# Heads' weight blocks before units', one period of 128 points, and the last piece of the first output block moved behind the second

## What is computed

```python
proj = jnp.einsum('btd,dc->btc', h, w_in[l])            # 4 * 1024 + 128 columns (rwkv), 4 * 1024 (hgrn)
o_rwkv = _rwkv7_branch(token_shift(proj[..., :RWKV_COLS]), ...)   # 16 heads of 64
o_hgrn = _hgrn2_branch(proj[..., RWKV_COLS:], ...)                # 8 heads of 128
y = jnp.einsum('btc,cd->btd', jnp.concatenate([o_rwkv, o_hgrn], axis=-1), w_out[l])
h = _layer_norm(ALPHA * h + y, ln_w[l], ln_b[l])
```

## Time and profile before

| | us |
|---|---|
| median of 3 runs | 3085.81 (3084.92 to 3086.78) |
| the profiled execution's own time | 3083.08 |
| its span | 3081.3 |
| TensorE busy in the span | 2990.8 (97%) |
| second block up to the second output block | 1789.11 to 2932.41 |

### The profile page before, as it was taken

One profiled execution on the slowest core, in us unless ns is written; L12 is line 12 of the kernel. 1 busy time (PEld: TensorE's weight loads), 2 busy tenths in 40 slices (PEclk: granted clock), 3 DMA queues, 4 the chain that ended last, 5 costly groups with the idle time before them and its releaser, 6 DMA issues.

```text
span 3081.3 us, 39125 instructions
## 1 busy us (share of the span) xinstructions
PE 2990.8 (97%) x15290; PEld 2418.7 (78%) x15290; DVE 1688.9 (55%) x2944; ACT 1244.6 (40%) x2150; POOL 284.5 (9%) x517
## 2 busy tenths in 40 slices
PE   8999999999999999999999999899999999999897
PEld 7778787787878887777778868787887887878786
DVE  6554545555543336566643364756666656564647
ACT  5443443434332335355442333344434343434422
POOL 0110101010100000000000011202112020212001
PEclk9999999999999999999999999999999999999999
DMA  4222222222234322222234322212223132224344
GB/s 166 78 81 83 83 77 82 83 82 76 83 127 144 105 89 70 77 74 70 75 137 140 104 90 70 84 62 78 90 63 98 55 92 66 80 76 143 132 130 157
DMA packets 86006, 288.97 MB, mean 94 GB/s; under 512 B 12080, under 2 KB 12720, under 8 KB 85568
## 3 DMA queue, kind: packets, MB, share of 16 engines
q1 hardware_dynamic: 69696, 243.66, 24.4%
q0 software_dynamic: 16128, 42.81, 4.5%
HBM read 261.13 MB, written 25.17 MB: 93 GB/s over the span
## 4 chain that ended last, share of the span: by engine, by line
PE 84%; DVE 8%; ACT 4%; issue 3%; DMA 1%; POOL 1%; DVEq 0%; SPq 0%; ACTq 0%; POOLq 0%
PE bank L280 15%; PE bank L282 14%; PE bank L281 14%; PE bank L284 7%; PE bank L286 7%; PE bank L285 7%; PE bank L1371 2%; PE bank L1302 1%; PE bank L1307 1%; PE bank L337 1%; PE bank L317 1%; DVE mc_split L735 1%; ACT mc_split L563 1%; PE bank L1282 1%; PE bank L466 1%
## 5 line engine op out<-in xcount | busy, mean ns | idle before, releaser
L280 PE MATMUL bank<-ma_split,mc_split 128*128 128x512 f32 x2304 | 956.3, 415 | 12.7 <-DVE ma_split L892 7.7
L735 DVE TENSOR_TENSOR mc_split<-mc,mc_split 128x1024 fp32r<-128x1024 f32 x434 | 535.2, 1234 | 783.4 <-ACT mc_split L563 782.4
L282 PE MATMUL bank<-ma_split,mc_split 128*128 128x512 f32 x2304 | 905.2, 393 | 0.0
L281 PE MATMUL bank<-ma_split,mc_split 128*128 128x512 f32 x2304 | 901.6, 391 | 0.0
L563 ACT ACTIVATE mc_split<-mc 128x1024 fp32r<-128x1024 f32 x434 | 457.5, 1055 | 650.6 <-PE bank L284 345.3
L280 PEld LDWEIGHTS bank<-ma_split,mc_split 128*128 128x128 f32 x2304 | 436.1, 189 | 121.2 <-issue 48.8
L282 PEld LDWEIGHTS bank<-ma_split,mc_split 128*128 128x128 f32 x2304 | 434.2, 188 | 97.0
L281 PEld LDWEIGHTS bank<-ma_split,mc_split 128*128 128x128 f32 x2304 | 436.6, 190 | 78.4 <-issue 4.2
L284 PE MATMUL bank<-mc_split,ma_split 128*128 128x512 f32 x576 | 230.2, 400 | 4.9 <-DVE mb L1781 3.4
L286 PE MATMUL bank<-mc_split,ma_split 128*128 128x512 f32 x576 | 225.3, 391 | 0.0
L285 PE MATMUL bank<-mc_split,ma_split 128*128 128x512 f32 x576 | 224.7, 390 | 0.0
(11 more groups left out here) (364 smaller groups left out, 3742.0 us busy)
## 6 DMA issues: line engine op xcount, KB each, us to landing
mc<-in_w SPq DMA_DIRECT2D x434, 512.0 KB, 3.5
x<-mc POOLq DMA_DIRECT2D x8, 1024.0 KB, 5.3
y<-mb_split SPq DMA_DIRECT2D x28, 256.0 KB, 2.5
ma_split<-y POOLq DMA_DIRECT2D x28, 256.0 KB, 4.4
mb<-in_xt SPq DMA_DIRECT2D x8, 512.0 KB, 9.0
mc<-in_x POOLq DMA_DIRECT2D x4, 1024.0 KB, 5.7
mc<-x POOLq DMA_DIRECT2D x4, 1024.0 KB, 8.1
mats<-mc POOLq DMA_DIRECT2D x32, 128.0 KB, 2.2
```

The source lines that it names most:

```text
L280: mm = pe.matmul(banks[j][:], wh[:, c], act_hi[:, kt, :], start=(kt == 0), stop=False)
L281: pe.matmul(banks[j][:], wl[:, c], act_hi[:, kt, :], start=False, stop=False)
L282: last = pe.matmul(banks[j][:], wh[:, c], act_lo[:, kt, :], start=False, stop=(kt == KT - 1))
L735: dve.tensor_tensor(w_low[:, s % NR, :, :], w_raw[:, s % NR, :, :], w_high[:, s % NH, :, :].bitcast(F32), ALU.subtract).then_inc(w_lo, 1)
```

## The change

It touches no product and no step's content. Four things move:

1. **Order of blocks.** Unit 0, `wa`, then head i and unit i + 1 in turn, then head 7: each head's block now stands ahead of the unit with the next number.
2. **Places of steps.** A unit's steps all begin at 128 u: prolog at 128 u + 10, V at + 32, G0 at + 42 (three points apart, before two), X at + 98, U0 at + 121, E0 at + 150. Before, prolog and chunks had periods of 128 and 120, so the distance between one unit's tail and the next unit's prolog shrank by 8 points a unit. A head's steps begin at 128 h + 65, 4.5 points apart, 4.0 for the last head (before 2.3 for head 6 and 2.0 for head 7).
3. **The first output block** has seven slots; its eighth, with the last unit's and last head's results, is a block of its own (`LATE`) behind the second output block. Its four banks are added by four more VectorE operations of 128 x 512.
4. **POOL's list.** Ten of the fourteen loads of earlier results (`y_loads`) stand ahead of the last unit's `sub_inverses`, and the rest, with two loads of the residual (`x2_load`), inside it.

```diff
-SLOT0 = [8 * b if b <= WA else 8 * b - 6 for b in range(BLOCKS)]
+LATE = OUT2 + 2
+BLOCKS = OUT2 + GROUPS + 1
+SLOTS = [2 if b == WA else 7 if b == OUT2 else 1 if b == LATE else 16 if b == BLOCKS - 1 else 8 for b in range(BLOCKS)]
+SLOT0 = [sum(SLOTS[:b]) for b in range(BLOCKS)]
...
-            KIND = [("rw", 0), ("wa", 0), ("rw", 1)]
-            for i in range(UNITS - 2):
-                KIND += [("hg", i), ("rw", i + 2)]
-            KIND += [("hg", i) for i in (UNITS - 2, UNITS - 1)] + [("out", n) for n in range(GROUPS)]
+            KIND = [("rw", 0), ("wa", 0)]
+            for i in range(UNITS - 1):
+                KIND += [("hg", i), ("rw", i + 1)]
+            KIND += [("hg", UNITS - 1), ("out", 0), ("out", 1), ("late", 0), ("out", 2), ("out", 3)]
...
-                i = k - CHUNKS
-                late = 0 if u else 5
+                i, begin = k - CHUNKS, 128 * u
                 if k < PART_B:
-                    return (128 * u - 54 if u else 7) + 2 * k
+                    return begin + 10 + 2 * k
                 if k < CHUNKS:
-                    return 120 * u + 16 + late + 2 * (k - PART_B)
-                begin = 120 * u + 26 + late
+                    return begin + 32 + 2 * (k - PART_B)
                 if i < 4:
-                    return begin + 2 * i
+                    return begin + 42 + 3 * i
                 if i < 13:
-                    return begin + 54 + 5 * (i - 4) // 2
+                    return begin + 98 + 5 * (i - 4) // 2
                 if i < CHUNK_K:
-                    return begin + 77 + 5 * (i - 13) // 2
-                return begin + 105 + 3 * (i - CHUNK_K)
+                    return begin + 121 + 5 * (i - 13) // 2
+                return begin + 150 + 3 * (i - CHUNK_K)
...
-                rate = {UNITS - 2: 23, UNITS - 1: 20}.get(h, 45)
-                return 64 * (BLOCK_OF["hg", h] + 1 - LANE0) + 1 + m * rate // 10
+                return 128 * h + 65 + m * (40 if h == UNITS - 1 else 45) // 10
...
+                    to = xr[0][:, t, :] if b == OUT2 else x3[:, t, n * N:(n + 1) * N]
+                    if b == LATE:
+                        dve.wait_ge(bank_free[t], freed(OUT2 + 1, t))
+                    dve.tensor_tensor(to, banks[t][:], xr[n % 2][:, t, :], ALU.add).then_inc(bank_free[t], 1)
...
+                if u == UNITS - 1:
+                    y_loads(pool, range(10, 12))
+                    pool.wait_ge(copies_ready, 2 * UNITS)
+                    for n in range(2):
+                        x2_load(pool, n)
...
+                for u in range(UNITS - 1):
+                    sub_inverses(pool, u)
+                y_loads(pool, range(10))
+                sub_inverses(pool, UNITS - 1)
```

More of the change, by code:

```diff
@@ L261, in swa_steps, with products @@
                 return [k for k in range(18) if swa_step_at(g, k) - 8 * s in points]
-            def products(pe, b, lhs_w, act_hi, act_lo, needs, slot0=None, tiles=range(4)):
-                for kt in range(KT):
-                    s = (SLOT0[b] if slot0 is None else slot0) + kt // 2
+            def products(pe, b, lhs_w, act_hi, act_lo, needs, slot0=None, tiles=range(4), kts=range(KT)):
+                for kt in kts:
+                    s = (SLOT0[b] if slot0 is None else slot0) + (kt - kts[0]) // 2
                     if kt % 2 == 0:
@@ L1152, in programs, with lane_steps @@
                     AT.setdefault(hg_at(u, m), ([], []))[1].append((u, m))
-            def lane_steps(b, points=range(8 * BLOCK_SLOTS)):
-                for point in points:
-                    rw, hg = AT.get(64 * (b - LANE0) + point, ((), ())) if b >= LANE0 else ((), ())
+            def lane_steps(b, points=None):
+                for point in range(8 * SLOTS[b]) if points is None else points:
+                    rw, hg = AT.get(8 * (SLOT0[b] - SLOT0[LANE0]) + point, ((), ())) if b >= LANE0 else ((), ())
                     yield from (("rw", u, k) for u, k in rw)
@@ L1416, in needs @@
                         if b == OUT2:
[L1417 to L1420, removed]
+                            pe.wait_ge(y_in[kt // 2], 64)
+                        if b == OUT2 + 1 and kt >= KT - 2:
+                            pe.wait_ge(y_rw_lo if kt == KT - 2 else y_h_lo, UNITS)
                     if kind == "wa":
@@ L1430, in second_pe @@
                         continue
-                    for point in products(pe, b, kind != "out", h_hi, h_lo, needs):
+                    kts = range(KT - 2) if b == OUT2 else range(KT - 2, KT) if kind == "late" else range(KT)
+                    for point in products(pe, b, kind in ("rw", "hg"), h_hi, h_lo, needs, kts=kts):
                         if b == RW0 and point % 8 == 3:
@@ L2017, in sub_inverses, with x2_load, y_loads @@
                 pool.wait_ge(xt_in, 16 * (u + 1))
[L2019 to L2028, removed]
+            def x2_load(pool, n):
+                pool.dma_start(xr[n % 2], a["x2"].rearrange("(t p) n -> p t n", p=P)[:, :, n * N:(n + 1) * N]
+                               ).then_inc(x2_in[n % 2], 16)
+                pool.dma_start(gb[n % 2], a["final_g"][:, n * N:(n + 1) * N].broadcast_to([P, N])).then_inc(x2_in[n % 2], 16)
+            def y_loads(pool, which):
+                for i in which:
+                    kt = Y_ORDER[i]
                     pool.wait_ge(w_free, SLOT0[OUT2 - 1] + i // 2 + 2)
@@ L2132 @@
     wa = w2[:, lo:hi].reshape(2, 8, P, P).transpose(0, 2, 1, 3).reshape(2, P, 2 * N)
-    parts = [w1, rw[0], wa, rw[1]]
-    for i in range(UNITS - 2):
-        parts += [hg[i], rw[i + 2]]
-    parts += [hg[UNITS - 2], hg[UNITS - 1], blocks(x["w_out_2"][0].reshape(KT, P, D)[Y_ORDER].reshape(D, D))]
-    parts.append(parts[-1][-BLOCK_SLOTS:])
+    parts = [w1, rw[0], wa]
+    for i in range(UNITS - 1):
+        parts += [hg[i], rw[i + 1]]
+    last = blocks(x["w_out_2"][0].reshape(KT, P, D)[Y_ORDER].reshape(D, D)).reshape(GROUPS, BLOCK_SLOTS, P, 2 * N)
+    parts += [hg[UNITS - 1], last[0, :-1], last[1], last[0, -1:], last[2], last[3], last[3]]
     w1 = np.concatenate(parts)
```

51 lines of the change are left out of this document (25 added, 26 removed).

## The result

The changed kernel takes 3120.85 us (median of 4 runs, 3120.24 to 3121.91), the kernel before 3086.3 beside it (4 runs, 3084.92 to 3090.56): ratio 1.0112 [1.0097, 1.0126]. It is slower, as forecast, but by 34.6 us and not by 16. The profiled execution took 3120.24 us with a span of 3117.8, so its span is 36.5 us longer than that of before.

The account below looks back on a forecast made before the run. TensorE, busy for 97% of the span, bounds the kernel; idle time and low clock go from 74 to 90 us, so 16 us on the profiled 3083.08 give 3099, and 2.7 for the median 3102 us; range 3092 to 3113.

Parts of the forecast that it names:

- seams: Points just behind a unit's block, where VectorE has take, tail and prolog at once; seven new ones, 10.9 us each, 76 us.
- Rival C: A unit's tail does not hold VectorE; seams keep only the wait behind the take: 47 us shorter, 3039; chance 0.08.
- rival A: Seams cost 3 us more each (late ScalarE split, POOL's list or one more bank claim): about 3123; chance 0.16.
- first half: the take: In each seam, O1 waits 1.9 us for VectorE's copy of U1, queued behind the take.
- second half: the tail: In each seam, TensorE's E3 waits 5.6 us for VectorE's E2 (44.6 less 39.0 us into the seam).
- the shared bank: The head's step 21, right behind E3, waits 0.9 us for the bank that ScalarE still reads.
- clock: Behind the waits of 5.6 and 0.9 us TensorE runs at 1.2 GHz for some 5 us: 2.5 us lost each seam.
- the inverse: X waits 1.2 us in each of eight units, 9.6 us; POOL's eight issues in the last inverse cost 1 us more.
- first unit: Eight more points between k7 and N, so the wait at N goes; 1 us stays.
- last head and last unit: At the end, 4.0 points a step with no prolog beside them: 1.5 us.
- the late piece: Four VectorE additions and a second pass of banks beside its 8 points: 0.5 us, 2 if something else holds VectorE.
- Idle in a new seam: Sum of three waits in one seam, at O1, E3 and step 21: 8.4 us, against 5.08 and 6.91 in two old ones.

Follow-up runs that it names:

- E0: No run but a kernel step, the first of a unit's tail (E0 to E5), VectorE work of 1.65 us in the prediction's replay.
- experiment 1: Changed kernel with E3 to E5 of units 0 to 6 eight points later: 3087.35 us, ratio 1.0006 to the kernel before.
- experiment 5: Changed kernel with the tail (E0 to E5) of units 0 to 6 behind the prolog and eight loads behind the last inverse: 3058.26 us, ratio 0.9907.
- experiment 6: Experiment 5 with U0 to O3 four points later, the last unit's tail beginning at + 154: 3047.68 us, ratio 0.9874.
- experiment 9: Experiment 6 with loads spread: six and the residual's ahead of the last inverse, four inside, four behind: 3044.21 us, ratio 0.9864.
- Experiment 3: Changed kernel with E0 and E1 on one eighth of their elements from the second unit on (result not the reference's): 3107.11 us, ratio 1.0074.
- experiment 4: Changed kernel with POOL's list as before the change, all loads of results behind the last inverse: 3150.18 us, ratio 1.0207.
- experiment 8: Changed kernel with the tail of units 0 to 6 five points later than in experiment 9's order of blocks, loads as in experiment 5: 3081.66 us, ratio 0.9988.
- experiment 10: Experiment 9 with U0 to O3 of units 0 to 6 nine points later than in the change, heads' step 15 three later: 3049.69 us, ratio 0.9881.
- 2: Changed kernel with E2 of every unit one point earlier: 3106.01 us, ratio 1.0064.

## Why the prediction was right in direction and wrong in size

The direction and the mechanism stand. The seams took what the end gave back, and the wait of E3 for E2 is the largest in the second block. Moving E3 away from E2 (experiment 1) removes the whole loss. Rival C, at 3039 for this kernel, was no error in kind: the same order of blocks comes near it once the tail does not meet the prolog (3058, 3048 and 3044 in experiments 5, 6 and 9), which the change did not do. The measured time lies beside rival A's 3123. Of the causes that A names, one was there, one more bank claim in a row (the wait at the head's step 20); ScalarE's split and POOL's list were not late.

The size was wrong by a factor of two. The prediction had 90 us of idle time and low clock after the change. The trace shows 82.5 us of waits, and the 36.5 us by which the span grew over 74 put the sum at 110, so some 28 us are low clock. The granted clock read directly says the same: in the second block up to the end of the late piece TensorE is busy for 57.3 us at 0.50, and half of that, 28.7, is lost (before: 32.3 us, 16.2 lost, where the prediction took 18). By the terms of the sum:

| term | forecast | measured | off by |
|---|---|---|---|
| *first half: the take*, O1, seven | 13.3 | 14.6 | + 1.3 |
| the head's step 20, seven | none | 10.1 | + 10.1 |
| *second half: the tail*, E3, seven | 39.2 | 38.3 | - 0.9 |
| *the shared bank*, seven | 6.3 | 6.1 | - 0.2 |
| *clock*, in seams | 17.5 | 23 | + 5.6 |
| *the inverse*, and POOL's issues | 10.6 | 5.1 | - 5.5 |
| *first unit* | 1 | 4.4 | + 3.4 |
| *last head and last unit* | 1.5 | 3.2 | + 1.7 |
| *the late piece* | 0.5 | 0.7 | + 0.2 |
| low clock outside the pattern of the seams | none | 5 | + 5 |

The wait at step 20 is half of the 20 us by which the prediction's 90 are short, and the two lines of the clock are the other half. The other lines cancel, which is luck: the inverse was put 5.5 us too high, and the first unit, O1 and the end as much too low.

**The step that failed** is "Idle in a new seam: 1.9 + 5.6 + 0.9 = 8.4 us": it counts three waits where there are four. The replay followed VectorE's queue up to E2 and compared with TensorE only there. Its own figures had step 19's update end at 35.1 and TensorE at E3 at 39.0. TensorE comes to step 20 four points and a step, 3.7 us, before E3 (2538.63 to 2542.33), so at 35.3, and needs ScalarE's copies, 0.6 us behind the update's end (2538.01 to 2538.63): a wait of 0.4 us was in the replay and was not read off. The old seam's 1.90 us was this very wait, one step further on, where E0 then stood ahead of the update; E0 was moved up, and its wait moved with it. Experiment 3 shows it: with E0 0.93 us shorter, this wait is 0.94 us shorter. The rest of the 1.4 is that VectorE was 1.3 us later than replayed: it waited 1.17 us for TensorE at step 18's update (2530.40, 28.8 into the seam instead of 27.3) and ended step 19's at 36.4. At E3 the two errors met: VectorE later by 1.4, TensorE by the wait of 1.4 and a little more, so the 5.6 us came out right by luck.

**Clock.** This is the second term that was too small. The step "2.5 us for each seam" was taken from behind a single wait of 6.40 us. Two waits, 5.5 and 0.9, with only E3's four short matmuls between them, keep the low level for 6.8 us, and it costs 3.3 us by experiment 9. In two of the seven seams it had fallen behind O1's wait of 2.1 us as well. The clock also fell outside seams, in the blocks from 2729.96 (0.98) and 2882.19 (0.95), behind waits of 3.8 and 3.2 us; the prediction gave those parts waits of 1.2 and 1.5 and no clock. Of the 57.3 us of busy time at 0.50, 47.6 lie in the seams and 9.75 in these two places, so 23.8 and 4.9 us are lost there.

**The inverse.** "A wait of 1.2 us for each of eight units" was taken from one unit's 0.50 and a window one point shorter. Only four of eight X waited, three by 0.7 us or less and one by 3.8 us, where the inverse took longer to land. The point less is free in most units.

**First unit.** The wait at N is 0.7 us, as forecast, but the next turn, B's, waits 2.8 us for VectorE and the first block starts 0.9 late. I had looked only at N.

**Right:** E3, the shared bank, O1, the late piece (0.7 us with the second output block's start; the third output block takes 43.62 us, 43.52 before), and POOL's eight issues beside the way of the blocks (the last unit's X waits 0.5 us). On the table load: ScalarE switches only once there, for E1 and not for k7. Behind this load, at 2539.12, ScalarE stood idle for VectorE for 3.43 us, and VectorE's split began 1.54 us behind the state update, as in before. Nothing is late by the 1.4 us of drain that the Trainium skill, "ScalarE: Activation LUTs", What ACT_TABLE_LOAD costs, adds to a switch, though idle time at this place could hide it. Behind the load of the earlier trace rows, where nothing could, there is none: the next operation starts 0.01 us later.

Open is why the inverse of the seventh unit lands late in some kernels (a wait of 3.4 to 3.8 us at its X in the changed kernel and in experiments 1, 4, 5, 8, 9 and 10, 0.7 us or less in 2, 3 and 6). In the changed kernel the last transfer of that inverse lands in 6.2 us, where the median is 4.7; no run says why. With the low clock behind it this wait is worth some 4 to 5 us between versions, an estimate, and experiment 9 has it where 6 has not.

## What to carry to other kernels

When steps of two lanes share an in-order engine, replay the whole meeting, and at every instruction of the waiting engine compare both clocks, not only at the one that looks worst; a wait that had disappeared at one step stood here at the step before. The distance between the points where one lane's tail and the next lane's prolog stand was worth more here than the work in them: the same operations cost 9.9, 4.8 to 6.4 or 3.1 us of TensorE's idle time with the tail 12, 17 or 26 points behind. When the order of blocks changes, ask which transfers in another engine's queue were timed by the old order: here that was worth 29 us.

## What the runs showed of the hardware

**Two short waits cost less clock than one of 2.4 us.** 1.3 and 1.6 us, 5.7 us apart, left the granted clock at 1.00 in six of seven seams (experiment 9). One of 2.4 us brought it down in six of seven seams (experiment 10) and cost up to 3.0 us more than the wait. 2.4 us at step 21 brought it down in all seven (experiment 1).

**The same wait does not always cost the same, and its length does not set the price.** In one execution of experiment 10, seams with identical waits took 71.86, 73.44 or 74.90 us. O1's wait of 2.1 us is the same in the changed kernel and in experiments 1, 5 and 8, and the clock fell behind it in 2, 5, 4 and 5 of the seven seams. The 2.7 us at step 21 in experiment 8 brought it down in only two of seven. In experiment 9 it fell once behind a wait of 1.4 us, at 2188.36.

**The scatter between runs is only in part the clock's.** Over its ten runs kernel 1 scatters by 8 us, and the mean granted clock goes from 0.990 in the fastest to 0.988 in the slowest; 0.002 of 3088 us is 6 us, an estimate. Kernel 8 scatters by 16 us with a mean clock of 0.992 or 0.991, which is worth 3 us or, with the rounding, at most 6: where the rest comes from no run shows.
